# Two late gathers split into uneven parts, and the first tokens' output stored after the last gather

## The reference

```
top_s, top_i = lax.top_k(s, 16)                     # per token, 8 heads, two key halves
best_s, best_c = lax.top_k(all 16 x 16 sums, 16)    # 16 experts per head, 128 per token
expert = i1 * 128 + i2                              # a row of tables u and v, 16384 x 1024
act = gelu(einsum('thkd,td->thk', u[expert], xt))
h  += einsum('thk,thkd->td', softmax(best_s) * act, v[expert])
gate = sigmoid(rmsnorm(h) @ ple_gate_w);   out = h + (p @ ple_proj) * gate
```

## Time and profile before

| what | value |
|---|---|
| median of three executions | 1087.12 us |
| the profiled execution's own time | 1087.19 us |
| its span, and time around it | 1085.4 us, 1.8 us |
| PE, DVE, ACT, POOL busy | 92%, 63%, 42%, 29% of the span |
| DMA moved | 347.31 MB, of it 269.89 MB by POOL's gathers |
| written to memory | 1.05 MB, the output |

### The profile page before, as it was taken

How to read it: one execution, slowest core, us unless ns; L and a number is a source line. 1 busy time by engine, 2 the same in 40 slices (tenths; PEclk the granted TensorE clock), 3 DMA queues, 4 the chain that set the end, 5 groups by cost and what they waited for, 6 DMA issues and landing times.

```text
span 1085.4 us, 11222 instructions
## 1 busy us (share of the span) xinstructions
PE 993.2 (92%) x3773; PEld 566.4 (52%) x3773; DVE 688.2 (63%) x1555; ACT 460.3 (42%) x1201; POOL 317.2 (29%) x307
## 2 busy tenths in 40 slices
PE   9998999999999999999899698998788988877878
PEld 8998668444795565644454253555333432222324
DVE  5879556223553489787686676766458668667553
ACT  1253356111363157554644534445254364344333
POOL 4000000010000044445454334353434544443430
PEclk9999999999999999999999899999899999999999
DMA  9434442334627279999999999999999999999990
GB/s 354 169 135 186 155 155 78 123 118 167 242 90 309 103 295 421 421 415 422 422 420 421 421 420 422 420 421 421 422 421 420 421 422 413 421 422 420 418 416 33
DMA packets 46827, 347.31 MB, mean 320 GB/s; under 512 B 5073, under 2 KB 6481, under 8 KB 9265
## 3 DMA queue, kind: packets, MB, share of 16 engines
q0 software_dynamic: 37584, 269.89, 60.1%
q1 hardware_dynamic: 9184, 76.69, 18.6%
HBM read 345.25 MB, written 1.05 MB: 319 GB/s over the span
## 4 chain that ended last, share of the span: by engine, by line
PE 54%; DMA 29%; DVE 9%; ACT 6%; issue 2%; POOL 0%; DVEq 0%; POOLq 0%; ACTq 0%
DMA xc_rg<-in_peer_uv,small 20%; PE pp L1206 16%; PE pp L752 5%; DMA tail<-in_peer_uv,small 4%; PE pp L748 4%; PE pp L710 3%; DMA ig<-in_peer_uv,small 3%; PE pp L879 3%; PE pp L669 3%; PE pp L857 3%; PE pp L899 3%; DMA spare<-in_peer_uv,small 2%; PE pp L1096 2%; PE pp L706 2%; PE pp L1318 2%
## 5 line engine op out<-in xcount | busy, mean ns | idle before, releaser
L1681 ACT ACTIVATE small<-small 128x1 f32<-128x1 f32 x256 | 51.6, 202 | 319.0 <-DVE small L2462 318.0
L1695 ACT ACTIVATE diag<-ident,small 128x128 f32<-128x128 f32 x256 | 102.8, 402 | 8.4
L1206 PE MATMUL pp<-gl,diag 128*128 128x512 f32 x128 | 65.6, 637 | 21.2 <-ACT diag L1695 21.1
L1687 ACT ACTIVATE small<-small 128x1 f32<-128x1 f32 x256 | 75.4, 294 | 9.3
L1206 PE MATMUL pp<-sm,diag 128*128 128x512 f32 x128 | 64.3, 624 | 11.3 <-ACT diag L1695 11.3
L1206 PE MATMUL pp<-ig,diag 128*128 128x512 f32 x128 | 63.6, 620 | 10.1 <-ACT diag L1695 10.1
L1206 PE MATMUL pp<-kT,diag 128*128 128x512 f32 x128 | 63.4, 618 | 9.1 <-ACT diag L1695 9.1
L1206 PE MATMUL pp<-xc_rg,diag 128*128 128x512 f32 x128 | 61.6, 604 | 10.3 <-ACT diag L1695 10.3
L621 POOL DMA_INDIRECT ig<-in_peer_uv,small x32 | 40.2, 1257 | 105.0 <-PE pa L1161 53.6
L1206 PE MATMUL pp<-tail,diag 128*128 128x512 f32 x128 | 61.7, 604 | 9.1 <-ACT diag L1695 9.1
L1206 PE MATMUL pp<-spare,diag 128*128 128x512 f32 x128 | 62.7, 613 | 7.5 <-ACT diag L1695 7.5
(11 more groups left out here) (556 smaller groups left out, 2028.3 us busy)
## 6 DMA issues: line engine op xcount, KB each, us to landing
ring<-in_wall SPq DMA_DIRECT2D x31, 2048.0 KB, 7.9
ring<-in_wall SPq DMA_DIRECT2D x3, 512.0 KB, 7.0
ring<-in_wall SPq DMA_DIRECT2D x1, 1280.0 KB, 9.6
xs<-in_x SPq DMA_DIRECT2D x2, 512.0 KB, 3.7
post_g<-in_rows POOLq DMA_DIRECT2D x2, 512.0 KB, 8.5
tail<-in_wall SPq DMA_DIRECT2D x1, 1024.0 KB, 10.8
kT<-in_wall SPq DMA_DIRECT2D x1, 1024.0 KB, 12.8
lt<-in_sub_keys SPq DMA_DIRECT2D x1, 1024.0 KB, 8.2
```

The costliest lines, as they stand in the source:

```text
L1206: return nc.tensor.matmul(acc[t][:, c, :], diag[:, n * P:(n + 1) * P], rows_uv[page_of(g)][:, D + c * HALF:D + (c + 1) * HALF], start=Fals ...
L1681: nc.scalar.activation(acts[:, at:at + BATCH], dots[:, at:at + BATCH], ACT.Gelu_apprx_tanh)\
L1687: ins = nc.scalar.activation(wk[:, g % LAG:g % LAG + 1], acts[:, g % LAG:g % LAG + 1], ACT.Copy, scale=probs[:, g:g + 1])
L1695: nc.scalar.activation(diag[:, n * P:(n + 1) * P], ident[:, :], ACT.Copy, scale=wk[:, g % LAG:g % LAG + 1]).then_inc(s["diag_made"], 1)
```

## The change

1. Slot 236 is gathered in three indirect DMAs, for tokens 0 to 104, 105 to 106 and 107 to 127 of the tile; slot 238 in two, 0 to 119 and 120 to 127. All other slots stay one DMA. All of a slot's DMAs raise the same semaphore, and DVE waits for the larger count (`landed`).
2. A gather reads its row numbers from the first partition on. So SP copies the numbers of slots 228 to 239 from partitions 105 on, 107 on and 120 on, 12 columns each, to the first partitions of a free stretch `rest` of small2: three small DMAs of 23, 21 and 8 partitions with 48 bytes each. SP waits for `chosen` to reach 17 (head 14's numbers) ahead of them, and POOL waits for all three ahead of slot 236.
3. SP then waits for `piece_here` of slots 254 and 255 before its first store. The five stores keep their order and sizes.
4. The two semaphores of the first query weights become one; PE waits for both halves before either.

```
+SPLIT = {236: ((0, 105), (105, 107), (107, 128)), 238: ((0, 120), (120, 128))}
+REST_BASES = (105, 107, 120)
+REST_FROM, REST_COLS = 228, 12
+
+def landed(g):
+    more = sum(len(ranges) - 1 for n, ranges in SPLIT.items() if n <= g and page_of(n) == page_of(g))
+    return 16 * (landing_of(g) + more)
...
+        rest = small2[:, 1449:1449 + len(REST_BASES) * REST_COLS].bitcast(U32)
...
-                    sp.dma_start(first_queries[0], ...).then_inc(s["queries_kept0"], 16)
+                    sp.dma_start(first_queries[0], ...).then_inc(s["queries_kept"], 16)
                     sp.wait_ge(s["recur_ready"], 1)
-                    sp.dma_start(first_queries[1], ...).then_inc(s["queries_kept1"], 16)
+                    sp.dma_start(first_queries[1], ...).then_inc(s["queries_kept"], 16)
...
             parts = [(0, 0, HALF), (0, HALF, D)] + [(1, a, b) for a, b in LAST_PARTS]
+            sp.wait_ge(s["chosen"], REST_FROM // TOPK + 3)
+            for n, base in enumerate(REST_BASES):
+                sp.dma_start(rest[0:P - base, n * REST_COLS:(n + 1) * REST_COLS],
+                             experts[base:P, REST_FROM:REST_FROM + REST_COLS]).then_inc(s["rest_moved"], 16)
+            for n in range(LAST):
+                sp.wait_ge(piece_here[n], 16)
             for n, (t, a, b) in enumerate(parts):
                 sp.wait_ge(s["y_made"], n + 1)
...
+                if g == min(SPLIT):
+                    pool.wait_ge(s["rest_moved"], 16 * len(REST_BASES))
...
-                nc.gpsimd.indirect_dma_start(out=rows_uv[page_of(g)], out_offset=None, in_=peer_uv,
-                                             in_offset=bass.IndirectOffsetOnAxis(ap=experts[:, g:g + 1], axis=0))\
-                    .then_inc(row_here[page_of(g)], 16)
+                for a, b in SPLIT.get(g, ((0, P),)):
+                    at = REST_BASES.index(a) * REST_COLS + g - REST_FROM if a else 0
+                    which = rest[0:b - a, at:at + 1] if a else experts[0:b, g:g + 1]
+                    nc.gpsimd.indirect_dma_start(out=rows_uv[page_of(g)][a:b, :], out_offset=None, in_=peer_uv,
+                                                 in_offset=bass.IndirectOffsetOnAxis(ap=which, axis=0))\
+                        .then_inc(row_here[page_of(g)], 16)
...
-                    pe.wait_ge(s[f"queries_kept{n}"], 16)
+                    pe.wait_ge(s["queries_kept"], 16 * len(first_queries))
...
-                dve.wait_ge(row_here[page_of(g)], landing_of(g) * 16)
+                dve.wait_ge(row_here[page_of(g)], landed(g))
```

More of the change, by code:

```diff
@@ L123 @@
         "att_turned", "att_moved", "ao_full", "ao_used", "nsa_osums", "nsa_ostd", "nsa_out", "mix_turned",
-        "mixT_made", "mixed_full", "sums_copied", "sums_turned", "sums_gained", "rstd_made", "wp_used", "wo_full", "keys_loaded", "second_loaded", "queries_kept0", "queries_kept1", "hg_full", "query_full", "query_moved",
+        "mixT_made", "mixed_full", "sums_copied", "sums_turned", "sums_gained", "rstd_made", "wp_used", "wo_full", "keys_loaded", "second_loaded", "queries_kept", "rest_moved", "hg_full", "query_full", "query_moved",
         "pscore_full", "pscore_moved", "ple_moved",
@@ L456, in _ @@
                     sp.wait_ge(s["bias2_made"], 1)
-                    sp.dma_start(first_queries[0], wall[UNIT_AT["wq0"]][:, 0:2 * D]).then_inc(s["queries_kept0"], 16)
+                    sp.dma_start(first_queries[0], wall[UNIT_AT["wq0"]][:, 0:2 * D]).then_inc(s["queries_kept"], 16)
                     sp.wait_ge(s["recur_ready"], 1)
-                    sp.dma_start(first_queries[1], wall[UNIT_AT["wq0"]][:, 2 * D:4 * D]).then_inc(s["queries_kept1"], 16)
+                    sp.dma_start(first_queries[1], wall[UNIT_AT["wq0"]][:, 2 * D:4 * D]).then_inc(s["queries_kept"], 16)
                 if name == "wq0":
```

## The result

The changed kernel took 1099.44 us, median of 4 runs (1098.38 to 1099.97), against 1087.62 us for the kernel before (1086.24 to 1088.46): ratio 1.0109, interval 1.0091 to 1.0126. It is slower by 12 us; I had forecast 3.3 us less.

A forecast was written before the change was run, and what follows sets the result against it. The expert stage was taken as bound by gather landings, set by one lagging DMA engine. 1087.19 - 1.24 (stores) - 2.17 (uneven gathers) = 1083.78, given as 1083.8 us; range 1082.5 to 1086.6.

The forecast's parts named there:

- The uneven gathers: Slots 236 and 238: odd row counts give late engines fewer rows, every landing from slot 238 on 2.17 us earlier.
- The relief: Slots 236 and 238 take 7 rows off the laggard, the engine 4 to 5 us behind the crowd: 2.17 us.
- the first rival: Slots 236 and 238: the laggard's share stays at 16 or rises to 18; 1085.95 or 1086.57 us; chance 0.24.
- The slower rival: Slots 236 and 238: odd counts fall on few engines, 105 rows on one, 30 us; about 1112 us; chance 0.06.
- a gap of many us at slot 236: Sign in the expert stage that the prediction was wrong because few engines got the odd row counts.
- The stores: First tile's stores, moved from slot 188 to behind slot 255: 1.24 us less, new place costs nothing.
- POOL, copies, query weights: Three more gather issues on POOL, SP's copies of row numbers, the joined wait for query weights: each costs nothing.
- the rounded-up rival: Slots 236 and 238: rows dealt in rounded-up shares, gain 0.9 us; 1085.05 us with the stores, or 1084.6; chance 0.08.

The follow-up runs named there:

- the pair with partitions 32 to 95 and 0 to 63: Stores moved late, slots 236 and 238 gather only those 64 partitions' rows, against the kernel before: 1084.72 us (32 to 95) and 1092.88 us (0 to 63).
- 64 and 64: Stores moved late, slots 236 and 238 each gathered as 64 and 64 rows, against the kernel before: 1096.59 us, ratio 1.0087.
- two halves of 128 partitions: Stores moved late, slots 236 and 238 each gathered as two DMAs of 128 rows of 4 KB, against the kernel before: 1086.64 us, ratio 0.9994.
- the last experiment: Stores moved late, slots 236 and 238 gather only rows 32 to 89, as 56 and 2, against the kernel before: 1083.66 us, ratio 0.9956.

## Why the prediction was wrong

**The uneven gathers** are the step that failed. I put them at -2.17 us; they cost 12.9 by the dots. I worked out how many rows each engine gets and left out where it writes them. The evidence for what stands in its place is the pair with partitions 32 to 95 and 0 to 63 (8.1 us apart), and the pair 64 and 64 against two halves of 128 partitions (10.5 us apart): the loss hangs on partitions, not on the count of gathers, row counts or moved starts. The ends of my range for this term were a gain of 4.97 and a loss of 0.62 and, as a rival, 30 us; no row of the trace before has a DMA of fewer than 128 partitions in the full stream, so the honest bound on the loss side was a stream at half rate for as long as engines are inside, and I never formed it. The prediction draws on what the Trainium skill says of dealing rows to engines, and not on what it says of where they are written.

By the Trainium skill's port rule, quoted above, the sizes of the change fit too; this is argued, as no trace tells the engines apart. 120 rows are 8 neighbouring ones per engine, and engines 4 apart then share their ports (the first and the fifth, the second and the sixth); 105 gives 7 apiece across the borders. A whole gather is dealt otherwise: the Trainium skill, DMA: Bandwidth & Descriptors, "The descriptor swizzle", gives engine 0 partitions 0 to 3 and 32 to 35, and so on, one port for each. No run here shows that dealing directly; a stream of whole gathers runs near 421 GB/s here.

**The relief** of the laggard is not seen. The end of the windows after:

```profile
1070.00:1071.00 1.00, 1.00 (x3) 0.19 (x1) 0.65 (x2) 0.28 (x2) 0.00 (x0) 1.00 0.16 66
1071.00:1072.00 1.00, 0.50 (x2) 0.30 (x2) 0.13 (x1) 0.62 (x2) 0.00 (x0) 1.00 0.12 49
1072.00:1073.00 1.00, 1.00 (x3) 0.38 (x2) 1.00 (x1) 0.00 (x0) 0.00 (x0) 1.00 0.13 45
1073.00:1074.00 1.00, 0.69 (x2) 0.00 (x0) 0.97 (x3) 0.80 (x3) 0.00 (x0) 1.00 0.07 29
1074.00:1075.00 1.00, 0.85 (x2) 0.49 (x3) 0.98 (x3) 0.64 (x4) 0.00 (x0) 1.00 0.07 29
1075.00:1076.00 1.00, 1.00 (x4) 0.40 (x3) 0.61 (x2) 0.68 (x3) 0.00 (x0) 1.00 0.06 25
```

One engine alone (0.07 of 16 is 1.1) runs from 1073 to past 1076, over 3 us where it was 1.5. From the crowd's end to the last packet the tail takes some 7.4 us (1068.9 to 1076.3) where it took 5.3 (1058.5 to 1063.8), about 2 more; with the 10.5 us of lost stream that makes 12.6 of the 12.9 (two windows behind those eight, at 395 and 350 GB/s, lose some 0.9 more, so the sum is good to about 0.6). The even split of 64 and 64, which leaves every engine its 8 rows, has a tail just as long (1065.0 to 1072.3 us). So the longer tail comes with the collisions, and no relief shows on top of it. The engine that was to lose the most rows, 7, the sixteenth from where the dealing starts, isn't the laggard by the dots of the last experiment. Whether the laggard was the eighth, which was to lose 5, or one that was never relieved, as the first rival has it, stays open.

**The slower rival** had the sign and not the mechanism. It had one engine loaded and the others idle; the windows show all 16 busy. Its mark, "a gap of many us at slot 236", is wrong too: the gaps begin at slot 233, three slots ahead of the first uneven gather, and the rate falls between 1004 and 1008 us, when slot 236's first piece had been issued at 1002.06 and slot 233 was still to land, at 1011.9. My reading is that the engines ahead were already in slot 236 while the laggard was in 233.

**The stores:** -1.24 predicted, -1.24 and -1.26 by the dots, -1.75 by the medians, with an interval of 0.3 to 2.6 less. In their new place they cost nothing.

**POOL, copies, query weights** cost nothing, as said. POOL's pieces follow each other by 2.2 us after the first and 1.2 after the others, instead of 1.53, and it waited for PE, not for the copies, ahead of slot 236:

```profile
1002.06 1.92 POOL L646 DMA_INDIRECT xc_rg<-in_peer_uv,small  x1 [2.13 <-PE pp L1231]
1004.28 0.88 POOL L646 DMA_INDIRECT xc_rg<-in_peer_uv,small  x1 [0.30 <-issue]
1005.46 0.93 POOL L646 DMA_INDIRECT xc_rg<-in_peer_uv,small  x1 [0.30 <-issue]
```

**A slip in a sum:** the rounded-up rival's 1084.6 should be 1087.19 - 1.24 - 1.5 = 1084.45. Nothing else hangs on it.

## What to carry to other kernels

When a stream of DMAs is the bound, keep its DMAs spread over the ports: all 128 partitions, or, by the Trainium skill's rule and the run here, a stretch like 32 to 95. Cutting a row range costs more than its rows, since it slows all that is in flight; cut along the free dimension (the bytes of a row) instead, which cost 0.1 us here. Read the DMA share and the rate side by side: a full share at half the rate is a collision, a low share is a wait.

## What the runs showed of the hardware that I had not expected

A badly placed DMA slows the whole gathers beside it as much as itself. At 1008 to 1012 us after the change the rate is 193 GB/s over all 16 engines, while the landing of that time is that of a whole slot, 233. The loss therefore doesn't follow the rows: 8.1 us for one split slot, 12.9 for two near each other, 8.1 for half the rows of two slots. I read it as following how long any engine is inside, which the spread of the engines stretches; no run varies that spread.

A lagging engine need not be a slow one. Alone in the tail, the last engine moved about 26 GB/s (29 GB/s at a share of 0.07 of 16), against 421 / 16 = 26.3 in the full stream. The share stays near 1.00 while slots land every 2.48 us, so no engine waits for the laggard. Its distance over many slots isn't seen directly, as the trace doesn't name engines.

PE's granted clock fell to 0.50, the 1.2 GHz level, from 1016 to 1020 us and from 1032 to 1036; ahead of both PE had stood idle 3.1 and 1.9, then 3.0 and 1.8 us before its products. Four products of slot 237 then took 3.60 us instead of 1.98:

```profile
1032.80 3.60 PE L1231 MATMUL pp<-gl,diag 128*128 128x512 f32 x4 [1.78 <-ACT diag L1720]
1037.39 1.98 PE L1231 MATMUL pp<-ga,diag 128*128 128x512 f32 x4 [0.98 <-ACT diag L1720]
```

It cost nothing, as the gathers were later still.
